# The sample tokens' high and low parts side by side in one stationary operand

## The reference

```python
def one_block(xt):
    q = (xt @ w_q).reshape(PEER_BLOCK, PEER_HEADS, 2, PEER_HALF)
    ...
    eidx = jnp.take_along_axis(cidx, pos, axis=-1)
    gate = jax.nn.softmax(sc, axis=-1)
    act = jax.nn.gelu(jnp.einsum('thkd,td->thk', e_u[eidx], xt).astype(jnp.float32))
    w = (gate * act).astype(xt.dtype)
    return jnp.einsum('thk,thkd->td', w, e_v[eidx])
...
y_prompt = rms_norm(hp, norm_final_g)
y_sample = rms_norm(hs, norm_final_g)
```

## Time and profile before

| what | value |
|---|---|
| median of 3 runs | 4513.93 us (4512.45 to 4514.62) |
| profiled execution, whole time | 4513.97 us |
| its span (first to last instruction) | 4512.2 us |
| output phase, first to last matmul start | 2931.97 to 4504.20 us |
| granted TensorE clock, mean over the span | 0.961 |

### The profile page before, as it was taken

The page is one execution under the profiler, slowest core; times in us unless marked ns, Lnnn a source line. Parts: engine busy times, 40 slices in busy tenths (PEclk is TensorE's granted clock), DMA queues, the critical chain, the costliest instruction groups (busy, mean ns, idle before and its releaser), DMA issues.

```text
span 4512.2 us, 56756 instructions
## 1 busy us (share of the span) xinstructions
PE 4296.7 (95%) x22358; PEld 3710.3 (82%) x22358; DVE 2386.4 (53%) x4464; ACT 1284.9 (28%) x2696; POOL 404.7 (9%) x260
## 2 busy tenths in 40 slices
PE   6988878879999999999999999899999999999999
PEld 4556536669999999999999999878878878877887
DVE  2323212221179987588887885155555555555554
ACT  1122111111122222566666665211111111111111
POOL 0000000001112222111111111100000000000000
PEclk8888879859999999999999999999999999999999
DMA  4000120001122222343333344465555445554452
GB/s 175 0 0 0 50 125 20 19 26 43 38 78 87 93 92 87 120 156 152 151 151 151 151 157 156 152 184 131 136 133 138 131 131 136 134 137 131 131 136 78
DMA packets 383607, 484.73 MB, mean 107 GB/s; under 512 B 290688, under 2 KB 308616, under 8 KB 380104
## 3 DMA queue, kind: packets, MB, share of 16 engines
q1 hardware_dynamic: 381000, 411.43, 30.2%
q10 hardware_dynamic: 2448, 71.30, 3.7%
HBM read 329.78 MB, written 153.89 MB: 107 GB/s over the span
## 4 chain that ended last, share of the span: by engine, by line
PE 94%; DVE 2%; DMA 2%; ACT 1%; issue 1%; POOL 0%; DVEq 0%; ACTq 0%; SPq 0%; POOLq 0%
PE ps L318 47%; PE ps L976 38%; PE ps L1014 3%; PE ps L361 1%; PE ps L992 1%; PE ps L821 1%; DMA gate_in<-gates 1%; PE ps L783 1%; DMA win<-w_in 0%; PE ps L312 0%; PE ps L826 0%; DVE xT L559 0%; DMA vc_s<-vc 0%; PE ps L397 0%; PE ps L441 0%
## 5 line engine op out<-in xcount | busy, mean ns | idle before, releaser
L976 PE MATMUL ps<-xh,uh 128*128 128x364 f32 (+1 forms) x3456 | 1137.9, 329 | 8.1 <-POOL ul L1137 7.2
L976 PE MATMUL ps<-xl,uh 128*128 128x364 f32 (+1 forms) x3456 | 1137.0, 329 | 0.0
L976 PE MATMUL ps<-xh,ul 128*128 128x364 f32 (+1 forms) x3456 | 1135.8, 329 | 0.0
L318 PE MATMUL ps<-vh,wh 128*128 128x512 f32 (+1 forms) x2304 | 898.3, 390 | 15.0 <-DVE wl L1312 13.9
L318 PE MATMUL ps<-vh,wl 128*128 128x512 f32 (+1 forms) x2304 | 898.1, 390 | 0.0
L318 PE MATMUL ps<-vl,wh 128*128 128x512 f32 (+1 forms) x2304 | 897.0, 389 | 0.0
L1322 DVE TENSOR_TENSOR acc<-acc,ps 128x512 f32<-128x512 f32 (+1 forms) x576 | 393.8, 685 | 710.1 <-PE ps L318 710.1
L976 PEld LDWEIGHTS ps<-xh,uh 128*128 128x128 f32 x3456 | 651.0, 188 | 11.3 <-issue 10.1
L976 PEld LDWEIGHTS ps<-xl,uh 128*128 128x128 f32 x3456 | 650.8, 188 | 0.0
L976 PEld LDWEIGHTS ps<-xh,ul 128*128 128x128 f32 x3456 | 650.0, 188 | 0.0
L318 PEld LDWEIGHTS ps<-vh,wh 128*128 128x128 f32 (+1 forms) x2304 | 419.1, 182 | 120.4 <-issue 14.2
(11 more groups left out here) (214 smaller groups left out, 3826.5 us busy)
## 6 DMA issues: line engine op xcount, KB each, us to landing
hidden_after_gelu<-hid SPq DMA_DIRECT2D x128, 544.0 KB, 3.0
gates<-gs ACTq DMA_DIRECT2D x17, 4096.0 KB, 11.3
act_in<-hidden_after_gelu SPq DMA_DIRECT2D x128, 544.0 KB, 6.0
gate_in<-gates SPq DMA_DIRECT2D x128, 544.0 KB, 7.4
ur<-u_t SPq DMA_DIRECT2D x128, 512.0 KB, 4.4
vr<-v_w SPq DMA_DIRECT2D x128, 512.0 KB, 3.5
ur<-wq SPq DMA_DIRECT2D x16, 512.0 KB, 4.1
win<-w_in SPq DMA_DIRECT2D x1, 7168.0 KB, 22.5
```

What stands on the lines that cost most here:

```text
L318: i = nc.tensor.matmul(out, lhsT, rhs, start=(k == 0), stop=(k == len(pairs) - 1))
L976: i = nc.tensor.matmul(ps[:, h_bank(like, k), 0:w], lhsT, rhs, start=(m == 0), stop=(m == len(parts) - 1))
```

## The change

For the sample tile the high and the low parts of the weights stand side by side: columns 0 to 63 of a stationary operand are the high part, 64 to 127 the low part. A block of the sample tile then takes two matmuls (with `vh` and with `vl`), not three, and the product low x low comes with them. PSUM rows 0 to 63 and 64 to 127 hold two half sums, which `acc` keeps apart (its sample slot now has all 128 partitions, the upper half starting from zero). In the last quad, after ten groups, two fp32 matmuls with a stacked identity (128 x 64) add the halves; VectorE copies the result back. For this the weights' buffers are laid out anew (high part, then sample's low part, then the prompt's low part), the low part is subtracted in two instructions, the sample tile comes first in a quad and fifth in the final scaling, the accumulator's slots and loads are reordered to match, and TensorE's last two quads are straight code.

```diff
-    wh0 = sb("wh0", [128, QUAD, T], F32R)
+    w0a = sb("w0a", [128, 2, 2 * T], F32R)
+    stack = sb("stack", [128, SAMPLE])
...
-    wh1 = sb("wh1", [128, QUAD, T], F32R)
-    wl1 = sb("wl1", [128, QUAD, T], F32R)
+    w1 = sb("w1", [128, QUAD, 2 * T], F32R)
...
-    wl0 = sb("wl0", [128, QUAD, T], F32R)
+    w0b = sb("w0b", [128, 2, 2 * T], F32R)
+    def wboth(par, j):
+        return w1[:, j, :] if par else (w0a, w0b)[j // 2][:, j % 2, :]
+    O_ORDER = [NT] + list(range(NT))
+    Y_ORDER = [0, 1, 2, 3, NT, 4, 5, 6, 7]
+    def slot(t):
+        return (t + 1) % (NT + 1)
...
         for k in range(OGRP):
-            t, h = divmod(k, 2)
+            t, h = O_ORDER[k // 2], k % 2
...
-            parts = [(a[par][:, b, cols(t)], v_[par][:, b, h * 512:(h + 1) * 512])
-                     for b in range(QUAD) for a, v_ in ((wh, vh), (wl, vh), (wh, vl))]
-            mm_sum(ps[0:width(t), k % O_BANKS, :], parts, "output")
+            c = slice(h * 512, (h + 1) * 512)
+            if t == NT:
+                parts = [(wboth(par, b)[:, SEQ:SEQ + 2 * SAMPLE], v_[par][:, b, c]) for b in range(QUAD) for v_ in (vh, vl)]
+            else:
+                low = T + SAMPLE + t * 128
+                parts = [(wboth(par, b)[:, o:o + 128], v_[par][:, b, c])
+                         for b in range(QUAD) for o, v_ in ((t * 128, vh), (low, vh), (t * 128, vl))]
+            mm_sum(ps[:, k % O_BANKS, :], parts, "output")
+            if known(qd, NQUAD - 1) and k == 9:
+                sample_summed(e)
+    def sample_summed(e):
+        e.wait_ge(sem("added"), (NQUAD - 1) * OGRP + 2)
+        e.wait_ge(sem("stacked"), 1)
+        for h in range(2):
+            i = nc.tensor.matmul(ps[0:SAMPLE, 6 + h, :], stack[:, :], acc[:, slot(NT), h * 512:(h + 1) * 512], start=True, stop=True)
+        i.then_inc(sem("s_sum"), 1)
...
-        with e.Fori(2, NQUAD, 2) as qd:
+        with e.Fori(2, NQUAD - 2, 2) as qd:
             output_quad(e, qd, 0)
             output_quad(e, qd + 1, 1)
+        output_quad(e, NQUAD - 2, 0)
+        output_quad(e, NQUAD - 1, 1)
...
-        nc.vector.tensor_tensor(wl[par][:, j, :], act_in[:, b % 2, :], wh[par][:, j, :].bitcast(F32), ALU.subtract).then_inc(sem("w_lo"), 1)
+        w = wboth(par, j)
+        nc.vector.tensor_tensor(w[:, T:T + SAMPLE], act_in[:, b % 2, SEQ:T], w[:, SEQ:T].bitcast(F32), ALU.subtract)
+        nc.vector.tensor_tensor(w[:, T + SAMPLE:2 * T], act_in[:, b % 2, 0:SEQ], w[:, 0:SEQ].bitcast(F32), ALU.subtract).then_inc(sem("w_lo"), 1)
...
-        nc.vector.tensor_tensor(acc[0:p, t, c], acc[0:p, t, c], ps[0:p, k % O_BANKS, :], ALU.add).then_inc(sem("added"), 1)
+        nc.vector.tensor_tensor(acc[:, slot(t), c], acc[:, slot(t), c], ps[:, k % O_BANKS, :], ALU.add).then_inc(sem("added"), 1)
...
+        e.wait_ge(sem("u_lo"), NB)
+        nc.vector.memset(acc[SAMPLE:128, slot(NT), :], 0.0)
+        nc.vector.tensor_tensor(stack[:, :], ident[:, 0:SAMPLE], ident[:, SAMPLE:128], ALU.add).then_inc(sem("stacked"), 1)
+        e.wait_ge(sem("stacked"), 1)
         cuts = (0, 4, 9, 13, OGRP)
...
-        for t in range(NT + 1):
-            summed(e, NQUAD - 1, 2 * t)
-            summed(e, NQUAD - 1, 2 * t + 1)
-            if t >= 1:
-                scaled_out(e, t - 1)
+        for k in range(2):
+            summed(e, NQUAD - 1, k)
+        for i, t in enumerate(Y_ORDER):
+            if t == NT:
+                e.wait_ge(sem("s_sum"), 1)
+                for h in range(2):
+                    nc.vector.tensor_copy(acc[0:SAMPLE, slot(NT), h * 512:(h + 1) * 512], ps[0:SAMPLE, 6 + h, :]).then_inc(sem("s_whole"), 1)
+            else:
+                for h in range(2):
+                    summed(e, NQUAD - 1, 2 * t + 2 + h)
+            if i >= 1:
+                scaled_out(e, i - 1)
         scaled_out(e, NT)
...
             sp.wait_ge(sem("u_lo"), NB)
-            acc_in(0, 2, 0)
+            load(acc[0:SAMPLE, slot(NT), :], x3_d[SEQ:T, :], "acc_in_0")
+            acc_in(0, 1, 0)
             sp.wait_ge(sem("hidden"), NB * NG)
-            acc_in(2, 4, 1)
+            acc_in(1, 4, 1)
             load(fgain[:], final.partition_broadcast(128), "final_gain_in")
...
-            acc_in(6, NT - 6, 2)
-            load(acc[0:SAMPLE, NT, :], x3_d[SEQ:T, :], "acc_in_2")
+            acc_in(5, NT - 5, 2)
```

More of the change, by code:

```diff
@@ L1287, in o_act @@
             expert_high(e, b)
-        for t in range(NT + 1):
+        for i, t in enumerate(Y_ORDER):
             p = width(t)
-            e.wait_ge(sem("added"), (NQUAD - 1) * OGRP + 2 * t + 2)
-            need(e, "y_rstd", t)
-            if t == 0:
+            if t == NT:
+                e.wait_ge(sem("s_whole"), 2)
+            else:
+                e.wait_ge(sem("added"), (NQUAD - 1) * OGRP + 2 * t + 4)
+            need(e, "y_rstd", i)
+            if i == 0:
                 e.wait_ge(sem("w_lo"), PK)
-            nc.scalar.activation(ysq[0:p, :], acc[0:p, t, :], ACT.Square, accum_out=ssq[0:p, 0:1]).then_inc(sem("y_ssq"), 1)
+            nc.scalar.activation(ysq[0:p, :], acc[0:p, slot(t), :], ACT.Square, accum_out=ssq[0:p, 0:1]).then_inc(sem("y_ssq"), 1)
     def o_pool(e, ch):
-        for t in range(NT + 1):
+        for i, t in enumerate(Y_ORDER):
             p = width(t)
-            e.wait_ge(sem("y_ssq"), t + 1)
-            need(e, "y_scaled", t)
+            e.wait_ge(sem("y_ssq"), i + 1)
+            need(e, "y_scaled", i)
             rsqrt_mean(ch, ssq[0:p, 0:1], rst[0:p, 0:1], 1.0 / D, p, 0, 1).then_inc(sem("y_rstd"), 1)
@@ L1320, in summed, with scaled_out @@
             part = (0, 4, 12).index(k)
-            e.wait_ge(sem(f"acc_in_{part}"), 16 if part < 2 else 32)
-        nc.vector.tensor_tensor(acc[0:p, t, c], acc[0:p, t, c], ps[0:p, k % O_BANKS, :], ALU.add).then_inc(sem("added"), 1)
-    def scaled_out(e, t):
+            e.wait_ge(sem(f"acc_in_{part}"), 32 if part == 0 else 16)
+        nc.vector.tensor_tensor(acc[:, slot(t), c], acc[:, slot(t), c], ps[:, k % O_BANKS, :], ALU.add).then_inc(sem("added"), 1)
+    def scaled_out(e, i):
+        t = Y_ORDER[i]
         p = width(t)
-        if t == 0:
+        if i == 0:
             e.wait_ge(sem("final_gain_in"), 16)
-        e.wait_ge(sem("y_rstd"), t + 1)
-        if t >= 2:
-            e.wait_ge(sem(f"y_out_{t % 2}"), t // 2 * 16)
-        nc.vector.scalar_tensor_tensor(yo[0:p, t % 2, :], acc[0:p, t, :], rst[0:p, 0:1], fgain[0:p, :],
+        e.wait_ge(sem("y_rstd"), i + 1)
+        if i >= 2:
+            e.wait_ge(sem(f"y_out_{i % 2}"), i // 2 * 16)
+        nc.vector.scalar_tensor_tensor(yo[0:p, i % 2, :], acc[0:p, slot(t), :], rst[0:p, 0:1], fgain[0:p, :],
                                        op0=ALU.mult, op1=ALU.mult).then_inc(sem("y_scaled"), 1)
@@ L1569, in acc_in @@
             def acc_in(t, n, part):
[L1570 removed]
+                load(acc[:, slot(t):slot(t) + n, :], x3_d[t * 128:(t + n) * 128, :].rearrange("(t p) d -> p t d", p=128), f"acc_in_{part}")
             sp.wait_ge(sem("u_lo"), NB)
[L1573 removed]
+            load(acc[0:SAMPLE, slot(NT), :], x3_d[SEQ:T, :], "acc_in_0")
+            acc_in(0, 1, 0)
             sp.wait_ge(sem("hidden"), NB * NG)
[L1575 removed]
+            acc_in(1, 4, 1)
             load(fgain[:], final.partition_broadcast(128), "final_gain_in")
@@ L1578, in _ @@
                 sp.wait_ge(sem(f"hid_out_{k}"), PK // 2 * 16)
-            acc_in(6, NT - 6, 2)
-            load(acc[0:SAMPLE, NT, :], x3_d[SEQ:T, :], "acc_in_2")
+            acc_in(5, NT - 5, 2)
             for b in range(NB - TURN, PK):
                 expert_in(b)
-            for t in range(NT + 1):
-                sp.wait_ge(sem("y_scaled"), t + 1)
-                load(y[t * 128:t * 128 + width(t), :], yo[0:width(t), t % 2, :], f"y_out_{t % 2}")
+            for i, t in enumerate(Y_ORDER):
+                sp.wait_ge(sem("y_scaled"), i + 1)
+                load(y[t * 128:t * 128 + width(t), :], yo[0:width(t), i % 2, :], f"y_out_{i % 2}")
             sp.wait_ge(sem("y_out_0"), (NT // 2 + 1) * 16)
```

8 lines of the change are left out of this document (3 added, 5 removed).

## The result

The new kernel takes 4456.84 us (median of 4 runs, 4455.81 to 4458.92) against 4514.16 us before (4 runs, the three of the table above and one more, 4512.45 to 4514.62). The ratio is 0.9874, 95% interval 0.9857 to 0.9891: 57.3 us less. The forecast was 4457.2 us, range 4451 to 4466. The profiled execution took 4457.24 us with a span of 4455.4 us.

The account below looks back on a forecast made before the run. TensorE's number of matmuls times their pace was taken to bound the output phase. 4513.97 - 58.7 (sample tile's matmuls) + 0.06 (first quad) + 1.9 (summing matmuls) = 4457.2 us, range 4451 to 4466 us.

Parts of the forecast that it names:

- The bound: Output phase: TensorE hardly waits, so the number of matmuls times their pace is the phase's time.
- Sample groups: Sample tile's matmuls: 16 wide instead of 24 narrow per quad, 3.63 against 5.52 us, 58.7 us less over 31 quads.
- Margins at a quad's turn: Between quads: the next quad's operands are ready 9.3 us before TensorE needs them, and this margin stays.
- (a): Rival at each quad's turn: a new wait takes the gain, a quad stays 49.04 us; 4516 us, chance 2%.
- (b): Rival in the sample tile's matmuls: reloading the same stationary slice shows by some 40 ns; 4477 us, chance 7%.
- (c): Rival in the sample tile's matmuls: reloading a slice in use can't be hidden, 0.415 us each; 4551 us, chance 2%.
- The split: VectorE's low-part subtraction in two instructions: 0.14 us extra per expert, hidden under VectorE's idle time.
- The first quad: Restart after six groups hangs on expert 4's gate transfer, so this quad gains nothing: +0.06 us, wait about 3 us.
- Summing matmuls and tail: Last quad's two fp32 matmuls count in full, 4 x 0.472 = 1.9 us; sum, scaling and store after the last group: 0.
- (d): The forecast itself holds: 87%, and 2% for smaller mishaps above the range that still leave it faster.

Follow-up runs that it names:

- before_both: Kernel before the change, with block 3's loads issued earlier and the first quad's first sums ahead of expert block 4: 4505.95 us.
- both: New kernel with block 3's loads issued ahead of the last hidden store and the first quad's first sums ahead of expert block 4: 4447.92 us.

## Why the prediction was right

**The bound.** Forecast: number of matmuls times their pace, nothing else in the phase. Shown: undoing the count alone gives the time of before back, filling the freed places with wide matmuls does the same, and neither more VectorE instructions nor another order of the blocks changes anything.

**Sample groups.** Forecast 16 x 0.2267 = 3.63 us and 31 x 1.89 = 58.7 us; measured 3.63 us and a quad of 47.15 us (49.04 before). Priced at the 215.7 ns that the forecast took from the Trainium skill ("TensorE: Matmul & The Clock Gate", Back-to-back issue gap), an estimate of 4462 us, the time would have come out 5 us above the measured one. The forecast left out that the same section gives about 131 ns for a matmul of 512 columns in a stream of load and matmul pairs, which is what this kernel issues; the pace of 226.7 ns in the rows is far from it. The pace taken from the rows gave the time to within 0.4 us.

**Margins at a quad's turn.** 9.3 us forecast, 9.1 measured, no wait in 31 quads. Rival (a) falls. Rivals (b) and (c), a price for loading the same slice again, fall by the pace of 0.2267 us and by the run with the slices apart.

**The split.** Forecast +0.14 us an expert, about twice what it turned out to be. In expert 4 the small subtraction starts at 2949.49 us and the large one at 2949.64 us:

```profile
2949.49 0.23 DVE L1344 TENSOR_TENSOR w<-act_in,w 128x64 fp32r<-128x64 f32 x1
2949.64 1.22 DVE L1345 TENSOR_TENSOR w<-act_in,w 128x1024 fp32r<-128x1024 f32 x1
```

The small one takes 0.15 us of VectorE's time, but the large one is shorter than the single one was. From the expert's start to the first sum are 2950.77 - 2947.02 = 3.75 us, against 2950.59 - 2946.91 = 3.68 us before: +0.07 us, near the forecast's lower bound of 0.06. Hidden it is, as the run with five pieces shows.

**The first quad.** The restart was forecast 0.14 us later and is 0.19 us later (0.11 by block 4's gates, 0.07 by the split), for the reason given: it hangs on block 4's gates, and these kept their place in the queue. With the 0.08 us that the wide groups behind it save, its net effect is 0.11 us (forecast 0.06). The picture of it was wrong in two sizes. The wait should have grown to about 3 us and is 0.6 us, because the phase started 1.27 us later (2933.24 against 2931.97) and because its first matmuls were slow for longer. Why it started later is shown in part: 0.3 us is the end of the hidden phase. The other 1.0 us is the way from there to the phase's start, 15.2 us against 14.3; it was 15.1 to 16.0 us in all profiled executions that have the new order of loads and block 3's loads in the old place. What makes it longer stays open; it cost nothing, since the restart doesn't hang on it. Windows of TensorE behind the start (columns as above):

```profile
2933.00:2937.00 4.00, 3.77 (x9) 3.02 (x10) 1.27 (x3) 0.00 (x0) 0.00 (x0) 0.50 1.03 412
2937.00:2941.00 4.00, 4.00 (x14) 3.12 (x14) 0.00 (x0) 0.00 (x0) 0.00 (x0) 0.70 1.02 410
```

The clock is at 0.50 (1.2 GHz) for the first four microseconds and for part of the next four; 14 matmuls stand 0.427 us apart, until 2939.34 us. In the kernel before the stretch was 3.9 us long (rows 4 have its window at 0.53). Both differences end in the wait in front of the restart, which is why the sum didn't feel them. Had the first sums stood ahead of expert 4, as in two of the runs above, they would have counted in full. The step held because of the queue, not because of the sizes that I gave it.

**Summing matmuls and tail.** 1.9 us forecast, 1.95 measured, though made up otherwise: 4 x 0.43 and 0.23 us for entering and leaving plain fp32, not 4 x 0.472. The forecast's lower bound for a record, 0.43 us, was the right price. The tail was put at 0 and gave 0.3 us back in the profiled execution (7.56 less 7.24 us), all of it behind the start of the last scaling: the store of a full tile lands in 2.6 us and that of a half one in 2.9 us. The runs' spread of 3 us hides it.

One sum of chances in the forecast is off: (a), (b) and (c) together are 11%, and 13% only with the smaller mishaps of (d).

So the forecast of 4457.2 us against 4456.84 is closer than its parts deserve: the runs of the new kernel spread over 3.1 us, and an offset of 0.4 us is chance.

## What to carry to other kernels

Where one engine is busy without a gap at a constant clock, and its operands come with a margin of several microseconds, count its instructions and multiply by the distance between starts: a stationary operand of half the width costs what a full one costs, so two halves that share their moving operand belong side by side. Look for the fixed points: an edit between the phase's start and a wait on a transfer isn't worth anything until the transfer itself comes earlier, and what moves it may be another transfer in front of it in the same queue. And where executions differ by more than the effect that you look for, compare the traces from an event on that lies behind the scatter: here the medians were good to about 2 us, the times from the restart on to 0.1 us.

## What the runs showed of the hardware

- A stationary operand of 64 columns is 3 ns dearer per matmul than one of 128 (0.230 against 0.2267 us), in the kernel before and in the run with 24 narrow matmuls. Loading the same slice twice or three times in a row costs nothing: the pace is 0.2267 us in both, with loads of 188 ns.
- The slow stretch behind the same start lasted 3.9 us in the kernel before and 6.1 us in the new one, both after an idle time of 14 to 15 us. In the profiled executions of the experiments, whose waits at the start were 7.9 to 15.7 us, it held for 6 to 14 matmuls. At 0.427 instead of 0.227 us each that is a loss of 1.2 to 2.8 us. Behind the same wait of 7.9 us it lasted 3.0 us in one run (before_both) and 6.1 us in another (both), so the length of the wait doesn't explain it; what does stays open.
- A gap of 3.58 us in TensorE's stream, behind some 12 us without a break at the full clock, left the granted clock at 1.00.
- Plain fp32 matmuls of 512 columns at a granted clock of 1.00 cost 0.43 us a record, two records a matmul, and 0.23 us once for the whole stretch, however many there are (4 or 36 records).
